# Mixture of experts in a decoder trunk: an item's tokens fetched and stored by indirect DMA instead of gathered and scattered by matmuls

## The reference

```python
logits = jnp.dot(t, w_router)
top_logit, top_idx = lax.top_k(logits, TOP_K)          # TOP_K = 2
top_w = jax.nn.softmax(top_logit, axis=-1)
gate = jnp.einsum('tk,tke->te', top_w, one_hot(top_idx, N_EXPERTS))
for e in range(N_EXPERTS):                             # 8
    out = out + gate[:, e:e + 1] * swiglu(t, w_gate[e], w_up[e], w_down[e])
```

## Time and profile before

| | us |
|---|---|
| median of 3 runs | 1662.79 (1662.22 to 1664.09) |
| profiled execution, its own time | 1664.51 |
| its span | 1662.7 |
| TensorE busy | 1578.3 |
| VectorE busy | 1291.7 |
| ScalarE busy | 1028.2 |
| GpSimd busy | 14.4 |

### The profile page before, as it was taken

The page is one execution under the profiler, slowest core; times in us unless marked ns, Lnnn a source line. Parts: engine busy times, 40 slices in busy tenths (PEclk is TensorE's granted clock), DMA queues, the critical chain, the costliest instruction groups (busy, mean ns, idle before and its releaser), DMA issues.

```text
span 1662.7 us, 21462 instructions
## 1 busy us (share of the span) xinstructions
PE 1578.3 (95%) x8127; PEld 1339.4 (81%) x8127; DVE 1291.7 (78%) x1100; ACT 1028.2 (62%) x865; POOL 14.4 (1%) x36
## 2 busy tenths in 40 slices
PE   5998999999899769999999999999999999999996
PEld 4987788887788758888888888888888888888885
DVE  4976744458687566888888888888888888888885
ACT  3545543446354625767767767777677677677664
POOL 3000000000000000000000000000000000000000
PEclk9997999999899778999999999999999999999998
DMA  7431365556334037999999999999999999999970
GB/s 233 150 128 51 109 210 195 180 175 189 115 128 140 7 114 260 373 375 328 371 364 331 377 351 346 376 340 357 375 340 359 374 340 357 374 342 357 374 286 25
DMA packets 203182, 439.70 MB, mean 264 GB/s; under 512 B 12088, under 2 KB 31104, under 8 KB 203136
## 3 DMA queue, kind: packets, MB, share of 16 engines
q1 hardware_dynamic: 200080, 437.38, 74.4%
q10 hardware_dynamic: 3056, 1.68, 0.4%
HBM read 437.98 MB, written 1.05 MB: 264 GB/s over the span
## 4 chain that ended last, share of the span: by engine, by line
PE 86%; DVE 8%; ACT 3%; SPq 2%; issue 1%; DMA 0%; DVEq 0%; ACTq 0%
PE bank L1316 25%; PE bank L1318 25%; PE bank L1317 25%; DVE wlo L804 2%; PE bank L1654 2%; PE bank L1690 1%; PE bank L1393 1%; PE bank L1467 1%; SPq L395 1%; PE bank L1311 1%; PE bank L1671 0%; PE bank L1672 0%; PE bank L1456 0%; ACT whi L519 0%; PE bank L1476 0%
## 5 line engine op out<-in xcount | busy, mean ns | idle before, releaser
L804 DVE TENSOR_TENSOR wlo<-raw,whi 128x2048 fp32r<-128x2048 f32 x415 | 935.5, 2286 | 147.8 <-ACT whi L709 94.3
L709 ACT ACTIVATE whi<-raw 128x2048 fp32r<-128x2048 f32 x341 | 632.7, 1910 | 9.1 <-DMA raw<-in_w_exp_down_dram 6.7
L1316 PE MATMUL bank<-whi,uTh 128*128 128x512 f32 (+1 forms) x1312 | 516.9, 394 | 5.7 <-DVE uTl L858 4.8
L1318 PE MATMUL bank<-whi,uTl 128*128 128x512 f32 (+1 forms) x1312 | 510.0, 389 | 0.0
L1317 PE MATMUL bank<-wlo,uTh 128*128 128x512 f32 (+1 forms) x1312 | 509.4, 388 | 0.0
L1316 PEld LDWEIGHTS bank<-whi,uTh 128*128 128x128 f32 x1312 | 247.8, 189 | 55.8 <-issue 5.0
L1318 PEld LDWEIGHTS bank<-whi,uTl 128*128 128x128 f32 x1312 | 247.5, 189 | 51.7
L1317 PEld LDWEIGHTS bank<-wlo,uTh 128*128 128x128 f32 x1312 | 247.9, 189 | 48.4
L1316 PE MATMUL bank<-whi,hTr 128*128 128x512 f32 x528 | 206.1, 390 | 0.0
L1317 PE MATMUL bank<-wlo,hTr 128*128 128x512 f32 x528 | 205.5, 389 | 0.0
L1318 PE MATMUL bank<-whi,hTr 128*128 128x512 f32 x528 | 205.5, 389 | 0.0
(11 more groups left out here) (246 smaller groups left out, 1175.7 us busy)
## 6 DMA issues: line engine op xcount, KB each, us to landing
raw<-in_w_exp_gate_dram SPq DMA_DIRECT2D x112, 1024.0 KB, 5.2
raw<-in_w_exp_up_dram SPq DMA_DIRECT2D x112, 1024.0 KB, 5.2
raw<-in_w_exp_down_dram SPq DMA_DIRECT2D x112, 1024.0 KB, 5.0
raw<-in_w_in_dram SPq DMA_DIRECT2D x28, 1024.0 KB, 5.4
raw<-in_w_ffn_gate_dram SPq DMA_DIRECT2D x11, 1024.0 KB, 5.1
raw<-in_w_ffn_up_dram SPq DMA_DIRECT2D x11, 1024.0 KB, 5.1
raw<-in_w_ffn_down_dram SPq DMA_DIRECT2D x11, 1024.0 KB, 4.9
raw<-in_w_out_dram SPq DMA_DIRECT2D x8, 1024.0 KB, 4.9
```

What stands on the lines that cost most here:

```text
L709: nc.scalar.activation(whi[:, s % SPLIT, :], raw[:, s % RAW, :], ACT.Copy).then_inc(hi_a, 1)
L804: return V.tensor_tensor(wlo[:, n % RAW, :], raw[:, n % RAW, :], whi[:, n % SPLIT, :].bitcast(F32), ALU.subtract).then_inc(lo_ready, 1)
L1316: T.matmul(o, sth, mvh, start=start, stop=False)
L1318: return T.matmul(o, stl, mvh, start=False, stop=stop)
```

## The change

The tokens after the norm are written to a table in memory, `tok`, in two halves (one by ScalarE's queue, one by GpSimd's). For each item TensorE multiplies `sel` by a column that holds, for each token, the number of the row where this expert's result is to be stored, plus two (`rows_of_item`: two matmuls with one column). VectorE makes two index columns of it, `get_row` (the token) and `put_row` (a token has two rows in `ybuf`, for its first and second expert; unused places get rows of their own behind them). GpSimd fetches the 128 rows of the next item by indirect DMA into `xg`, TensorE transposes them eight times (`turn_tokens`), and ScalarE and VectorE split the result as they did. At the end of an item ScalarE copies the result to `ysb` and GpSimd stores it by indirect DMA. After the loop SyncE's queue loads `ybuf` back in two halves of 1 MB and VectorE adds both rows of each token, each times its gate, to `h`. `select` moves from chunk 35 to chunk 27.

```diff
         @block.sync
+            sp.wait_ge(scattered, n_items * 16 + 16)
+            for t in range(TT):
+                rows2 = ybuf[t * 2 * P:(t + 1) * 2 * P, :]
+                sp.dma_start(back[t], rows2.rearrange("(p k) n -> p k n", k=2)).then_inc(yb_in[t], 16)
         @block.gpsimd
+            def fetch(i, turns):
+                pool.wait_ge(pool_turn, turns)
+                pool.wait_ge(get_ready, i + 1)
+                nc.gpsimd.tensor_tensor(idle, spare, spare, ALU.add).then_inc(pool_turn, 1)
+                nc.gpsimd.indirect_dma_start(xg, None, tok, bass.IndirectOffsetOnAxis(ap=get_row, axis=0)).then_inc(xg_in, 16)
+            pool.wait_ge(un_ready, MOE_NORM * TT + 2)
+            nc.gpsimd.dma_start(tok[P:2 * P, :], un[:, 1, :]).then_inc(scattered, 16)
...
+            fetch(0, 1)
+            with pool.Fori(0, n_items) as i:
+                fetch(i + 1, i * 2 + 2)
+                pool.wait_ge(pool_turn, i * 2 + 3)
+                pool.wait_ge(put_ready, i + 1)
+                pool.wait_ge(y_ready, i * 2 + 4)
+                nc.gpsimd.tensor_tensor(idle, spare, spare, ALU.add).then_inc(pool_turn, 1)
+                nc.gpsimd.indirect_dma_start(ybuf, bass.IndirectOffsetOnAxis(ap=put_row, axis=0), ysb, None).then_inc(scattered, 16)
         @block.scalar
+            def y_out(i):
                 act.wait_ge(consumed, i * EXP_LOADS + (NSTATIC + EXP_LOADS))
+                act.wait_ge(scattered, i * 16 + 16)
                 for q in range(2):
-                    nc.scalar.activation(yeh[:, 4 * q:4 * q + 4, :], bank(5 + q, 4, P), ACT.Copy).then_inc(y_a, 1)
+                    nc.scalar.activation(ysb[:, q * NC:(q + 1) * NC], bank(5 + q), ACT.Copy).then_inc(y_ready, 1)
                     if n == LAST_UP:
+                        act.wait_ge(consumed, i * EXP_LOADS + (NSTATIC + LAST_UP + 1))
                         tokens_hi(i + 1, 0)
                         tokens_hi(i + 1, 1)
                         turn_hi(i, r)
         @block.vector
+            def rows_to_get(i):
+                dve.wait_ge(row_ps, i + 1)
+                link_row(V.tensor_copy(row_sb, bank(7)[:, 0:1]), 5 * i + 2)
+                link_row(V.tensor_scalar(get_row, row_sb, 2.0, -2.0, ALU.max, ALU.add), 5 * i + 3)
+                V.tensor_scalar(get_row, get_row, 1, None, ALU.logical_shift_right).then_inc(get_ready, 1)
+            def add_experts(t):
+                dve.wait_ge(yb_in[t], 16)
+                link(V.scalar_tensor_tensor(h[:, t, :], back[t][:, 0, :], g1[:, t:t + 1], h[:, t, :], ALU.mult, ALU.add))
+                V.scalar_tensor_tensor(h[:, t, :], back[t][:, 1, :], g2[:, t:t + 1], h[:, t, :], ALU.mult, ALU.add).then_inc(hacc, 1)
-                    if n in ADD_AT:
-                        add_expert(i, ADD_AT.index(n))
+                    if n == PUT_AT:
+                        rows_to_put(i)
+                    if n == SELECT_AT + 2:
+                        rows_to_get(i + 1)
-                y_lo(i)
-            for n in range(2):
-                add_last(0, n)
+            add_experts(0)
             norm(5, 0)
-            for n in range(2):
-                add_last(1, n)
+            add_experts(1)
         @block.tensor
+                        if r == 0 and hf == 0:
+                            pe.wait_ge(y_ready, i * 2 + 2)
-                    if n in COMBINE_AT:
-                        combine(i, COMBINE_AT.index(n))
+                    if n == SELECT_AT + 1:
+                        rows_of_item(i + 1)
+                    if n == LAST_UP - 1:
+                        turn_tokens(i + 1)
                     if n == LAST_UP:
-                        pe.wait_ge(comb_ready, i + 2)
-                        for q in range(2):
-                            gather(i + 1, q, unh, GATHER_HI, gath_hi)
                         turn(r)
-                        for q in range(2):
-                            gather(i + 1, q, unl, GATHER_LO, gath_lo)
-SELECT_AT = LAST_UP - 4
+PUT_AT = 6
+SELECT_AT = LAST_UP - 12
```

More of the change, by code:

```diff
@@ L226, in trunk @@
         exh = [region(1024 + 512 * i, NC) for i in range(2)]
[L227 to L230, removed]
+        sel = region(2048, TT, P)
+        xg = region(4096, D)
+        ysb = region(5120, D)
+        back = [region(4096 + 2048 * t, 2, D) for t in range(TT)]
         gainrow = region(8192, D)
@@ L247, in trunk @@
         at = [0]
+        tok = nc.dram_tensor("tok", [SEQ, D], F32).ap()
+        ybuf = nc.dram_tensor("ybuf", [2 * SEQ + P, D], F32).ap()
         def stat(n):
@@ L268, in trunk @@
         iitem = stat(4)
-        gcur = stat(TT)
+        row_of, spare, row_sb, unused, idle = stat(TT), stat(1), stat(1), stat(1), stat(1)
+        get_row, put_row = (small[:, at[0] + k:at[0] + k + 1].bitcast(U32) for k in range(2))
+        at[0] += 2
         assert at[0] <= 512
@@ L446, in _ @@
                            allow_small_or_imprecise_dtypes=True).then_inc(consts, 1)
+            for t in range(TT):
+                nc.gpsimd.iota(row_of[:, t:t + 1], pattern=[[0, 1]], base=2 + 2 * P * t, channel_multiplier=2,
+                               allow_small_or_imprecise_dtypes=True).then_inc(rows_known, 1)
+            nc.gpsimd.iota(spare, pattern=[[0, 1]], base=2 + 2 * SEQ, channel_multiplier=1,
+                           allow_small_or_imprecise_dtypes=True).then_inc(rows_known, 1)
             pool.wait_ge(zeroed, ZEROED)
@@ L738, in _ @@
             nc.scalar.activation(gexp, gdiff, ACT.Exp).then_inc(rexp, 1)
+            act.wait_ge(scattered, 16)
+            for q in range(2):
+                nc.scalar.activation(ysb[:, q * NC:(q + 1) * NC], ident[:, :].unsqueeze(1).to_broadcast([P, 4, P]), ACT.Copy).then_inc(y_ready, 1)
             act.wait_ge(table_ready, 1)
@@ L1164, in _ @@
             p_lo(1)
-            for t in range(TT):
-                V.memset(gcur[:, t:t + 1], 0.0).then_inc(y_d, 1)
             dve.wait_ge(rlog, 1)
@@ L1255, in _ @@
+            select(0)
+            rows_to_get(0)
+            dve.wait_ge(rexp, 1)
+            link(V.tensor_scalar(g1, gexp, 1.0, None, ALU.add))
+            link(V.reciprocal(g1, g1))
+            link(V.tensor_tensor(g2, gexp, g1, ALU.mult))
             for q in range(2):
@@ L1646, in _, with rows_of_item, turn_tokens @@
             n_items = pe.value_load(item_expert[0:1, ITEMS:ITEMS + 1], min_val=NE, max_val=ITEMS)
[L1648 removed]
+            def rows_of_item(i):
                 pe.wait_ge(sel_ready, i * 2 + 2)
[L1651 to L1674 removed]
+                for t in range(TT):
+                    last = T.matmul(bank(7)[:, 0:1], sel[:, t, :], iitem[:, 2 + t:3 + t], start=t == 0, stop=t == TT - 1)
+                last.then_inc(row_ps, 1)
+            def turn_tokens(i):
+                pe.wait_ge(xg_in, i * 16 + 16)
+                for q in range(2):
+                    for c in range(4):
+                        k = 4 * q + c
+                        last = T.transpose(bank(TOKENS[q], 4, P)[:, c, :], xg[:, k * P:(k + 1) * P], ident[:, :])
+                    last.then_inc(xT_ps, 1)
+            rows_of_item(0)
             pe.wait_ge(pT_rd[1], 1)
[L1676 to L1679 removed]
+            turn_tokens(0)
             with pe.Fori(0, n_items) as i:
@@ L1740, in _ @@
             pe.wait_ge(eul_ready, n_items * 2 + 2)
-            embed(1, tail_in(0), 0)
-            pe.wait_ge(comb_ready, n_items + 1)
-            pe.wait_ge(y_d, n_items * 2 + 2)
             for t in range(TT):
-                for n in range(2):
-                    scatter(4 + 2 * t + n, t, n)
-            embed(1, tail_in(0), 1)
+                embed(1, tail_in(0), t)
+            pe.wait_ge(y_ready, n_items * 2 + 2)
             norm(5, 0)
```

115 lines of the change are left out of this document (34 added, 81 removed).

## The result

| | before | after |
|---|---|---|
| median, same chip, 8 runs each | 1662.84 (1662.22 to 1664.26) | 1668.88 (1668.0 to 1673.65) |
| span of the profiled execution | 1662.7 | 1667.7 |

The changed kernel is slower: the ratio is 1.0038, with a 95% interval of 1.0028 to 1.0049. The forecast was 1666.8.

The account below looks back on a forecast made before the run. TensorE's instruction stream was taken to bound the item loop, and latency chains the start and end. Loop -12.2, clock falls +4.6, start +1.8 and end +9.8 summed to +4.0, 1666.8 us; the forecast's own range was 1663 to 1671.

Parts of the forecast that it names:

- Work removed and added: TensorE, per item: gathers, scatter pairs and sel transposes go, token transposes and row-number matmuls come; work falls by 4.35 us.
- Stall of 3.2 from last up to first down: At an item's end, TensorE waits on the hidden block's chain through VectorE and ScalarE, 3.2 us; before, 3.93.
- Net of an item: In the loop, each item gets 1.52 us shorter after the stall is counted; -12.2 us for eight items.
- Clock falls: TensorE's clock halves after the stall at three of eight items, 1.5 us per stretch; +4.6 us.
- Start: From sel to the items' first product: row numbers, indirect fetch of 5.0 us, transposes, rounding; +1.8 us (+0.4 to +6.8).
- End: After the last item: indirect store, reload, longer adds, slow first gated products; +9.8 us (+8 to +15).
- The sum: Whole program: -12.2 + 4.6 + 1.8 + 9.8 = +4.0, giving 1666.8 us, 0.24% slower.
- Rival A: The clock never falls in the eight stalls: 1662.2 us, or 1659.0 with indirect transfers as fast as plain; chance 0.17.
- B: The clock falls at all eight items: +7.4, 1674.2 us; chance 0.11.
- C: GpSimd is slow to issue, an indirect transfer takes 10 us: start +5.0, end +5.5, 1677 us; chance 0.11.
- D: Transfers become the loop's bound at 358 GB/s: item 126 us, 34 us in all, 1700 us; chance 0.03.
- E: Fetched rows arrive late and TensorE waits at chunk 38 in every item; needs a fetch over 20 us; chance 0.03.

Follow-up runs that it names:

- reordered kernel: Changed kernel with its last chunks ordered gate 6, up 6, down 5, down 6, hidden block 6 in a second buffer; 1641.6 us, ratio 0.9869.
- filler: Changed kernel with nine dummy matmuls of 512 columns in TensorE's stall after the last up product; 1662.5 us, ratio 0.9995.
- cover: Changed kernel with the eight token transposes split, four before and four behind the hidden block's transposes, after the last up product; 1659.4 us, ratio 0.9986.
- store only: Changed kernel with tokens gathered by matmuls as before, results still stored by indirect transfer and summed at the end; 1660.5 us, ratio 0.9981.
- clear issue: Changed kernel with down 5 behind up 6, plus VectorE's last weight split of an item waiting for the indirect store's issue; 1639.1 us, ratio 0.9863.
- the fetch alone: Kernel before with tokens fetched by indirect transfer and transposed before the last up product, results still scattered by matmuls; 1677.0 us, ratio 1.0085.
- plain transfers: Changed kernel with both indirect transfers replaced by plain ones of 128 fixed rows, output not the reference's; 1673.9 us, ratio 1.0067.

## Why the prediction was right

Direction and size came out as forecast, 1668.9 for 1666.8, and the mechanism is the one that was named. That the sum is so near is in part luck, since misses of both signs cancel in it. Step by step:

- **Work removed and added, -4.35 an item.** Shown by the reordered kernel, where nothing else is left: -4.31.
- **Stall of 3.2 from last up to first down.** 3.16, with VectorE free at its start in seven of eight. Net of an item -1.53, forecast -1.52; that is the -12.2.
- **Clock falls, three of eight at 1.5, +4.6.** The one term that was clearly mis-sized: the price was right, the number not. Five of eight at 1.5, +7.6. No row of the kernel before gave the three; it was chosen between none and eight. The filler shows that idle time is the cause of the falls and that taking it away gives back 6.4 to 6.9. Why it is five was not settled: stalls of the same length and content come both with a fall and without. (The two stretches shown above don't rank them either: the one at 1232.40 starts 0.9 us ahead of its stall and the one at 1356.30 only 0.2.)
- **Start, +1.8.** +2.34. The fetch took 4.34 from issue and 5.07 with GpSimd's small operation ahead of it, for 5.2 in the sum, so the transfer was right; the transposes, the rounding and the rest took 3.57 from the transposes to the product, where 2.9 was put. About 1 us of it came back. The clock of the start rises to full at 632.8 before and at 631.9 after, so fewer products lie at half clock. Before, and then after:

```profile
632.43 0.59 PE L1316 MATMUL bank<-whi,uTh 128*128 128x512 f32 x1
632.85 0.40 PE L1317 MATMUL bank<-wlo,uTh 128*128 128x512 f32 x1
```

```profile
631.53 0.56 PE L1348 MATMUL bank<-wlo,uTh 128*128 128x512 f32 x1
631.93 0.39 PE L1349 MATMUL bank<-whi,uTl 128*128 128x512 f32 x1
```

- **End, +9.8.** Copy to gated product is 8.1 longer, and the first gated products at half clock cost 0.8 more, +8.9. The store took 3.4 where 4.5 was put, the reload 4.8 for 5.1. The time of copy to norm is 12.3, forecast 13.5. Here the profile of the changed kernel is at the lucky end: with the same steps it takes 12.8 to 13.4 in the kernels filler, cover, store only and clear issue, because GpSimd's small operation ahead of the store begins there inside a split of VectorE (last section).
- **The sum.** Falls 3.0 above the forecast, the longer stall 0.2 above, the slow clock of the start 1 below, the end 0.9 below, start 0.5 above: 1.8 above, and the median is 2.1 above. The span grew by 5.0 and not by 6.0, since in that execution all work ahead of the change was about 1 us earlier (`sel` reaches TensorE at 618.01, before at 619.12). That is variation: in the profiles of the changed kernel and of the edits to it that leave that part alone it is 616.4 to 619.3.
- **Slips in the working.** None of them moves the forecast. Rival A's limit for "faster", fetch and store together under 6.3, should be 6.8 (9.5 less the 2.7 from 1662.2 to 1659.5); they took 7.7. The sum with both transfers at 3.2 us is 1663.7, not 1663.6. Two to five falls with transfers of 4 to 6 us give 1664 to 1672 by the prediction's own terms, not 1663 to 1671.

The rivals: A (the clock holds) did not occur; the filler kernel shows what it would have been, 1662.5 for the 1662.2 written for it. B (falls at all eight) did not occur in any profile; five was the most. C, ten us for an indirect transfer, is ruled out by 4.34 and 3.36. D, the transfers as the bound, is ruled out by the 379 GB/s of the reordered kernel over 920 us. By that row the limit of about 358 GB/s between a core and its memory that the Trainium skill gives (DMA: Bandwidth & Descriptors, Where 436 GB/s comes from) is none here, with one core running. E did not occur: TensorE waits at no point for the fetched rows within the items. The estimate by the Trainium skill for such a transfer, 3.2 us (DMA: Bandwidth & Descriptors, Anatomy of one DMA — SWDGE (gpsimd) path), is near the store, 3.36 from issue, and 1.1 under the fetch, 4.34.

## What to carry to other kernels

Work on the bounding engine (the one that everything else waits for, here TensorE) can be the cover of a latency chain, a row of steps on other engines that it would have to wait for; then taking it away gives back only what it exceeds the chain by, here 0.8 of 3.56 us. Price a removal by what stands next to the removed rows, and when it leaves a hole, move other work into the hole in the same step: that turned +6 us into -21, and into -24 with the clear issue. A change with two halves is worth measuring in halves, since one can gain and the other lose. And a hole on TensorE can cost twice, once for itself and once for the clock behind it: here at five of eight, 1.5 us each. Look also at what a new order does to the other engines: in the kernel before it cost 10 us, on VectorE's side.

## What the runs showed of the hardware

An indirect transfer's issue on GpSimd takes 1.0 us, and 2.8 to 2.9 when it begins inside a VectorE operation with two operands in SBUF, the memory that the engines work on (the weight split, 2.29 us each): sixteen of sixteen stores in the two runs of the reordered kernel and the eight fetches within the items of the kernel with the fetch alone, but none of the eight stores in the changed kernel and none in the clear version, where VectorE was idle. A fetch that began 0.03 us ahead of such a split took 0.96, and one that began 0.24 behind its start took 2.90:

```profile
838.90 4.50 DVE L845 TENSOR_TENSOR wlo<-raw,whi 128x2048 fp32r<-128x2048 f32 x2 [0.46 <-ACT whi L748]
838.87 0.96 POOL L499 DMA_INDIRECT work<-tok,small  x1
...
1452.27 6.70 DVE L845 TENSOR_TENSOR wlo<-raw,whi 128x2048 fp32r<-128x2048 f32 x3 [0.46 <-ACT whi L748]
1452.51 2.90 POOL L499 DMA_INDIRECT work<-tok,small  x1 [0.42 <-POOL small L498]
```

GpSimd's small addition shows the same more simply. It takes 0.2 us with VectorE idle; where it begins inside a split it lasts until 0.05 us behind the split's end, 0.7 us in the filler kernel at all eight items and 1.2 in the cover kernel at seven of eight.

The Trainium skill, SBUF — State Buffer, section Who interferes with whom, has a rule that fits: a VectorE operation with two inputs in SBUF contends with GpSimd's reads, and the one that came first holds the port to its end. By that rule the reading of the list of rows is what waits, and the rows agree as far as GpSimd comes second. The other way round they show no wait: the split that began 0.03 us behind a fetch (838.90 above) took its usual time. That it is the list that is read is argued, not shown. In the kernel with plain transfers one issue began 0.05 us behind the start of a split, and took no longer than the others, so the list seems to make the difference, as far as one case tells:

```profile
1460.09 4.49 DVE L849 TENSOR_TENSOR wlo<-raw,whi 128x2048 fp32r<-128x2048 f32 x2 [0.46 <-ACT whi L752]
...
1460.14 0.58 POOL L502 DMA_DIRECT2D work<-tok  x1 [0.23 <-issue]
```
